# A hybrid trunk on one core: three mixer edits, other banks for the branch units, and another opening on TensorE

## The reference

```python
h = rms_norm(x, g_mix[l]);  u = h @ w_in[l]
y_pool = pool_mixer(u[..., OFF_POOL:OFF_CONV], pool_w[l], pool_scale[l])
y_conv = conv_module(u[..., OFF_CONV:OFF_Q], ...)   # GLU, 31 taps, LayerNorm, silu
y_attn = forgetting_attention(q, k, v, f_logit, ...) # 8 heads of 64, causal, with a bias per head and pair of tokens
gates = sigmoid(u[..., OFF_G:] + b_gate[l])          # 3 branches x 1024
merged = gates[0] * (y_pool @ w_br_pool) + gates[1] * (y_conv @ w_br_conv) + gates[2] * (y_attn @ w_br_attn)
x = x + merged @ w_out[l]
h = rms_norm(x, g_ffn[l])
x = x + (swiglu(h, ...) if l == 0 else moe_ffn(h, ...))   # dense 2816 wide, then top 2 of 8 experts, 3584 wide
```

## Time and profile before

| | |
|---|---|
| median of 3 runs | 1582.47 us (1580.74 to 1584.38) |
| the profiled execution's own time | 1584.88 us |
| its span, first to last instruction | 1583.1 us |
| granted TensorE clock, mean | 0.999 |
| TensorE matmul busy | 1566.5 us, 99% |
| VectorE busy | 1293.3 us, 82% |
| ScalarE busy | 1042.7 us, 66% |
| GpSimd busy | 32.8 us, 2% |

### The profile page before, as it was taken

The page is one execution under the profiler, slowest core; times in us unless marked ns, Lnnn a source line. Parts: engine busy times, 40 slices in busy tenths (PEclk is TensorE's granted clock), DMA queues, the critical chain, the costliest instruction groups (busy, mean ns, idle before and its releaser), DMA issues.

```text
span 1583.1 us, 22472 instructions
## 1 busy us (share of the span) xinstructions
PE 1566.5 (99%) x9385; PEld 1379.9 (87%) x9385; DVE 1293.3 (82%) x1137; ACT 1042.7 (66%) x957; POOL 32.8 (2%) x28
## 2 busy tenths in 40 slices
PE   9999999999999999999999999999999999999998
PEld 8999999999999998888888888888888888888887
DVE  6995885455898677998987988987988987988986
ACT  7546563344656568777677777777777777677675
POOL 1000200001000100000000000000000000000000
PEclk9999999999999999999999999999999999999999
DMA  9544555555554447999998999998999999999994
GB/s 318 183 134 145 180 182 187 185 185 187 161 159 140 157 157 270 357 366 358 376 369 325 372 371 361 371 372 322 374 370 357 372 373 338 364 360 378 364 364 184
DMA packets 182491, 453.12 MB, mean 286 GB/s; under 512 B 7168, under 2 KB 81024, under 8 KB 182272
## 3 DMA queue, kind: packets, MB, share of 16 engines
q1 hardware_dynamic: 182400, 451.82, 79.7%
HBM read 450.74 MB, written 1.05 MB: 285 GB/s over the span
## 4 chain that ended last, share of the span: by engine, by line
PE 93%; DVE 5%; ACT 1%; DMA 1%; issue 0%; SPq 0%; DVEq 0%; ACTq 0%
PE bank L317 29%; PE bank L318 28%; PE bank L319 28%; DVE w_low L307 2%; PE bank L1678 2%; PE bank L1656 1%; PE bank L1701 1%; DMA raw<-w_in 1%; ACT w_high L303 0%; PE bank L1411 0%; DVE y_low L814 0%; DVE h_full L804 0%; PE bank L1479 0%; PE bank L1457 0%; DVE h_low L797 0%
## 5 line engine op out<-in xcount | busy, mean ns | idle before, releaser
L307 DVE TENSOR_TENSOR w_low<-raw,w_high 128x2048 fp32r<-128x2048 f32 (+1 forms) x426 | 959.4, 2290 | 112.6 <-ACT w_high L303 111.8
L303 ACT ACTIVATE w_high<-raw 128x2048 fp32r<-128x2048 f32 (+1 forms) x426 | 804.4, 1919 | 157.4 <-DMA raw<-exp_w 155.8
L317 PE MATMUL bank<-w_high,hg_high 128*128 128x512 f32 x896 | 351.8, 393 | 1.4 <-DVE w_low L307 1.4
L319 PE MATMUL bank<-w_high,hg_low 128*128 128x512 f32 x896 | 349.1, 390 | 0.0
L318 PE MATMUL bank<-w_low,hg_high 128*128 128x512 f32 x896 | 348.9, 389 | 0.0
L317 PE MATMUL bank<-h_high,w_high 128*128 128x256 f32 x1024 | 290.8, 284 | 1.7 <-DVE h_low L797 1.6
L318 PE MATMUL bank<-h_low,w_high 128*128 128x256 f32 x1024 | 285.6, 279 | 0.0
L319 PE MATMUL bank<-h_high,w_low 128*128 128x256 f32 x1024 | 285.6, 279 | 0.0
L317 PEld LDWEIGHTS bank<-w_high,hg_high 128*128 128x128 f32 x896 | 168.3, 188 | 36.4 <-issue 1.2
L317 PEld LDWEIGHTS bank<-h_high,w_high 128*128 128x128 f32 x1024 | 194.1, 190 | 6.4 <-issue 3.8
L319 PEld LDWEIGHTS bank<-w_high,hg_low 128*128 128x128 f32 x896 | 168.2, 188 | 35.3
(11 more groups left out here) (296 smaller groups left out, 1591.6 us busy)
## 6 DMA issues: line engine op xcount, KB each, us to landing
raw<-exp_w SPq DMA_DIRECT2D x336, 1024.0 KB, 5.3
raw<-w_in SPq DMA_DIRECT2D x39, 1024.0 KB, 5.1
raw<-ffn_w SPq DMA_DIRECT2D x33, 1024.0 KB, 5.3
raw<-w_out SPq DMA_DIRECT2D x8, 1024.0 KB, 5.1
raw<-w_br_attn SPq DMA_DIRECT2D x4, 1024.0 KB, 5.0
raw<-w_in SPq DMA_DIRECT2D x2, 1056.0 KB, 7.5
raw<-w_br_pool SPq DMA_DIRECT2D x2, 1024.0 KB, 5.1
raw<-w_br_conv SPq DMA_DIRECT2D x2, 1024.0 KB, 4.8
```

What stands on the lines that cost most here:

```text
L303: nc.scalar.activation(slot(wh, c), slot(raw, c), ACT.Copy).then_inc(s["high_done"], 1)
L307: nc.vector.tensor_tensor(slot(wl, c), slot(raw, c), slot(wh, c).bitcast(F32), ALU.subtract).then_inc(s["split_done"], 1)
L317: pe.matmul(dst, lh, rh, start=start and i == 0, stop=False)
L319: last = pe.matmul(dst, ll, rh, start=False, stop=stop and i == len(terms) - 1)
```

## The change

- The branch units 21 to 32 go round banks 0, 1, 4, 5, 2 in place of 0, 1, 2. Unit 33 has bank 0 still, whose last owner is now unit 31 in place of unit 30.
- On ScalarE `attn_out` stands ahead of `gate_out` at n = 17, 19 and 21, and at n = 23 `gate_out(20)` stands right behind the layer norm's tanh, ahead of the copy of the conv branch.
- `pair_scores` starts with q by k, adds both diagonal masks in one matmul of 2 x 128 columns, and ends with the bias rows.
- The last of the four zero matmuls ahead of the dense layer's sums, that of bank 7, stands behind the sums.
- At the start 22 matmuls of 512 columns take the place of 15 and the block of 24 of several widths.

```diff
-UNIT_BANK = [0, 1, 2, 4, 5, 0, 1, 2, 4] + [u % 3 for u in range(9, UNITS - 1)] + [1]
+UNIT_BANK = [0, 1, 2, 4, 5, 0, 1, 2, 4] + [u % 3 for u in range(9, 21)] + [0, 1, 4, 5, 2, 0, 1, 4, 5, 2, 0, 1] + [0, 1, 2, 1]
...
                         nc.scalar.activation(cs[:], cv[:], ACT.Tanh, scale=0.5).then_inc(s["ln_th"], 1)
+                        gate_out(20)
                         act.wait_ge(s["y_full"], 2 * l + 2)
                         nc.scalar.activation(yH[:, 2:4, :], yf[:], ACT.Copy).then_inc(s["y_high_done"], 1)
                         attn_out(3)
                         attn_high(3)
-                        gate_out(20)
...
+                    if n in (17, 19, 21):
+                        attn_out((n - 17) // 2)
                     if 12 <= n <= 22:
                         gate_out(n - 3)
-                    if n in (17, 19, 21):
-                        attn_out((n - 17) // 2)
...
                     for a in range(2):
-                        B = bank[4 + a]
-                        pe.matmul(B[:, 0:384], sel8[:, 2 * j + a:2 * j + a + 1].to_broadcast([P, P]), crow[:], start=True, stop=False)
-                        pe.matmul(B[:, 0:128], identr[:], maskr[:], start=False, stop=False)
-                        pe.matmul(B[:, 256:384], identr[:], maskr[:], start=False, stop=False)
+                        rows = slice(64 * a, 64 * a + 64)
+                        pe.matmul(bank[4 + a][:, 0:128], qk[rows, j, 0:P], qk[rows, 4 + j, 0:P], start=True, stop=False)
                     for a in range(2):
                         rows = slice(64 * a, 64 * a + 64)
-                        pe.matmul(bank[4 + a][:, 0:128], qk[rows, j, 0:P], qk[rows, 4 + j, 0:P], start=False, stop=False)
+                        pe.matmul(bank[4 + a][:, 128:384], qk[rows, j, P:S], qk[rows, 4 + j, :], start=False, stop=False)
                     for a in range(2):
-                        rows = slice(64 * a, 64 * a + 64)
-                        pe.matmul(bank[4 + a][:, 128:384], qk[rows, j, P:S], qk[rows, 4 + j, :], start=False,
+                        pe.matmul(fold(bank[4 + a][:], 2)[:, :, 0:P], identr[:], maskr[:].unsqueeze(1).to_broadcast([P, 2, P]),
+                                  start=False, stop=False)
+                    for a in range(2):
+                        pe.matmul(bank[4 + a][:, 0:384], sel8[:, 2 * j + a:2 * j + a + 1].to_broadcast([P, P]), crow[:], start=False,
                                   stop=True).then_inc(s["scores"], 1)
...
-                            for m in range(4):
+                            for m in range(3):
                                 zero_bank(4 + m)
                             norm_stats(1)
+                            zero_bank(7)
...
-            keep_awake(15, 7, wh[5][:, 0:P], wh[5][:, 0:512])
-            still = hH[:, 0:2, :].rearrange("p a b -> p (a b)")
-            for n in (512, 128, 264, 384):
-                pe.matmul(bank[7][:, 0:n], wh[5][:, 0:P], still[:, 0:n], start=True, stop=True)
-                for at in (0, 0, P, 0, 0):
-                    pe.matmul(bank[7][:, 0:S], wh[5][:, at:at + P], still[:, 0:S], start=True, stop=True)
+            keep_awake(22, 7, wh[5][:, 0:P], wh[5][:, 0:512])
```

## The result

The kernel after takes 1578.76 us in the median of 20 runs (1571.61 to 1581.2); the kernel before, run beside it, 1586.03 us (20 runs, 1579.69 to 1590.75). The ratio is 0.9948 with a 95% interval of 0.9936 to 0.9959: 8.2 us less by the ratio, 7.3 by the two medians. The forecast was 5.8 us, 0.9963: the side is right, the size somewhat small. By the time alone rival (1) with its 7.4 us, 0.9953, would fit better, and the forecast lies outside the interval; only the traces can tell the two apart.

What follows compares the result with a forecast made beforehand. The prediction took TensorE to bound the kernel, with 93% of the chain that ended last. Values 2.3, banks 2.5 and scores 1.0 make 5.8 us, from 1582.47 to 1576.7 us, own range 1575.2 to 1578.4.

Steps and rivals of the forecast that it cites:

- rival (1): At the banks, VectorE does not lag, so they give 4.1 us; 7.4 us in all, 1575.1 us; chance 0.25.
- Values: 1.14 a layer: In pair_turn(3), copying values earlier removes the second three transposes' stall: 1.14 us a layer, 2.3 in two.
- idle + 0.17 + 0.11: For TensorE's waits, a stall costs more than its row's idle time: add 0.17 and 0.11 us.
- Banks, the removed stalls: 2.05 a layer: At units 23, 26 and 28, five banks remove stalls of 0.74, 0.64 and 0.67: 2.05 us a layer.
- Banks, given back: 0.8: At unit 33, TensorE stalls 0.7 with refill on merged_low, the next split takes 0.1, leaving 1.25 us a layer.
- near 3 us long: Sign to look for: VectorE's w_low split beside GpSimd's adds would be near 3 us long.
- (2): At the merge, VectorE's lag takes all the banks give; 3.3 us gained in all, 1579.2 us; chance 0.14.
- (3): VectorE sets the end of the merge, its lag growing past the whole gain; time 1586 us; chance 0.04.
- Scores: 0.5 a layer: In the pairs' score blocks, the reorder saves about 0.5 us a layer, 1.0 in two; bounds 0 and 2.0.
- Zeros and start: 0: At the dense layer's sums and the kernel's start, no gain: TensorE starts 0.8 us earlier but waits until 18.1.
- rival (4): At the start, TensorE's pauses drop the clock to 1.2 GHz; 1.3 us of gain, 1581.2 us; chance 0.05.
- Rival (5): The change fails: other waits replace those removed, or the masks cost double; 1582.5 us; chance 0.06.

Runs made afterwards that it cites:

- experiment 1: Kernel before with only attn_out moved ahead of gate_out at n = 17, 19, 21; 1583.11 us, ratio 0.9986.
- experiment 2: Kernel before with only the new bank table and gate_out(20) behind the tanh; 1583.62 us, ratio 0.9983.
- Experiment 10: Kernel after with a small memset in place of each of GpSimd's four adds, conv part not merged; 1573.55 us, ratio 0.9933.
- experiment 6: Kernel after with gate_out(20) back behind attn_high(3) as before; 1574.54 us, ratio 0.995.
- experiment 5: Kernel after with the first output piece's w_low split ahead of branch(25); 1578.74 us, ratio 0.9951.
- 9: Kernel after with the first output piece's split ahead of branch(25) and GpSimd's fourth add on VectorE behind branch(29); 1577.6 us, ratio 0.9942.
- experiment 3: Kernel before with only the scores reordered: q by k first, one mask matmul, bias rows last; 1583.68 us, ratio 0.9977.
- experiment 4: Kernel before with only the last zero matmul behind the sums and the new start; 1584.36 us, ratio 0.9993.
- experiment 11: Kernel after with the old zeros and old start, keeping values, banks and scores; 1579.54 us, ratio 0.9963.
- 12: Kernel after with the first output piece's split ahead of branch(25), two adds on GpSimd and two on VectorE; 1577.3 us, ratio 0.9931.
- 8: Kernel before run again unchanged for a second trace; 1585.54 us, ratio to itself 1.0005.
- 7: Kernel after run again unchanged for a second trace; 1572.7 us, ratio 0.9944.

## Why the prediction came out right

**Values: 1.14 a layer.** Measured 1.16 in either layer, read at the turn itself, and shown alone by experiment 1. The forecast took it from the distance of starts; its rule "idle + 0.17 + 0.11" would have given 1.25 here, where the matmuls are transposes of 128 columns.

**Banks, the removed stalls: 2.05 a layer.** Measured 2.10 and 2.08, and the same in experiment 2. For these the rule held: 0.75, 0.65 and 0.69 by it, 0.76, 0.64 and 0.70 measured.

**Banks, given back: 0.8.** Measured 0.87 and 0.85: 0.71 at unit 33 and the rest at the split behind it. That leaves 1.23 in either layer where I said 1.25. The mechanism was that of the forecast: the split of 3.06 us ("near 3 us long"), released at the end of GpSimd's second add, which came at 166.29. Experiment 10 takes the adds away and the stall goes; 6 takes VectorE's gain of 0.7 away and it doubles. Rival (1), no lag, falls with these, and so do (2) and (3), which wanted 2.05 or more. The Trainium skill, SBUF — State Buffer, "Who interferes with whom", says that GpSimd and a VectorE instruction with two SBUF inputs exclude each other instruction by instruction; the 3.06 and 2.28 us with and without the adds, and the 1.77 of experiment 5, agree. My expectations for experiments 5 and 9 used this rule for the split and forgot it for the add two rows on. (Of the eight adds in the earlier trace rows two are over 3.3 us long, one in each layer, and not one as the prediction has it; the argument stands.)

**Scores: 0.5 a layer.** Measured at the blocks 0.58 and 0.67 in the trace of after, 0.40 and 0.44 in experiment 3. TensorE's timeline after, pair 0 and pair 1, to be laid beside the earlier trace rows:

```profile
83.04 0.49 PE L1457 MATMUL bank<-h_full 64*128 64x128 f32 x4
83.34 0.63 PE L1460 MATMUL bank<-h_full 64*128 64x256 f32 x4
83.90 0.50 PE L1462 MATMUL bank<-mask_r,ident_r 128*128 128x256 f32 x2
84.24 0.52 PE L1465 MATMUL bank<-bias_rows,head_rows 128*128 128x384 f32 x2
...
95.57 0.49 PE L1457 MATMUL bank<-h_full 64*128 64x128 f32 x4
...
97.12 0.82 PE L1479 MATMUL bank<-cst,prob 128*128 128x128 f32 x6
```

The mask with repeated columns goes at full speed, 0.34 for two. Pair 1's block, first to next group, is 1.55 in place of 1.69.

**Zeros and start: 0.** TensorE's timeline of the start, after, beside the earlier trace rows:

```profile
2.15 7.98 PE L1298 MATMUL bank<-w_high 128*128 128x512 f32 x22 [2.15 <-DVE w_high L1274]
10.89 0.39 PE L317 MATMUL bank<-w_high,y_high 128*128 128x256 f32 x1 [0.76 <-DVE w_low L1279]
...
18.48 0.40 PE L317 MATMUL bank<-w_high,y_high 128*128 128x264 f32 x1 [0.80 <-DVE w_low L307]
```

The first product starts 0.22 earlier, not the 0.8 I had: its `w_low` was there 0.5 later than in the first trace of before. As forecast it doesn't matter: the second piece waits for VectorE (at 18.48; it stood at 18.16 before, and the forecast was 18.1). Behind both pauses the granted clock is 1.00 and a product steps by 0.12, so rival (4) falls. The trace of experiment 4 has nothing for the two edits together, and experiment 11 without them equals the kernel after; the 2.1 us between the upper groups of experiment 4 and before stay unexplained.

**The sum.** 5.8 us forecast, 5.82 over the two mixers in the traces. That the two agree to the hundredth is luck: the 5.82 hold 0.71 lost to a step outside the change, and 0.43 gained at the start and 0.2 behind the turn of layer 0, which no term has. The terms read at their own places make 2.3 + 2.5 + 1.25, about 6.0 us.

What the forecast lacked lies for the most part outside the change. The dense layer's step (-6.68) was drawn low in the profiled execution. It was drawn high in the output projection of layer 0 (+0.71, in both traces of after and in experiment 2, not in 5, 6, 9, 10, 11 and 12). One wait of the experts, at 1429.81, is in none of the other thirteen traces. In the many runs 8.2 us stand by the ratio, or 7.1 by groups. The 1.3 us above 5.8 stay open. The first trace of before lies 1.5 below the median of its own group (1584.88 against 1586.4), so other executions of that kernel may have waits that this trace doesn't show; that these make up the rest is argued and not shown.

The single parts show the same excess. Their 35 runs of before have 13 in a lower group (median 1580.7) and 22 in an upper one (1586.8). Upper group against upper group, experiments 1 to 4 are 3.7, 3.2, 2.2 and 2.1 us below before, where the terms read in their traces are 2.3, 2.5, 0.8 and 0. These four gains add up to more than the whole change. So the traces give the size of each part here, and the times of the runs confirm the side and no more. None of the 24 runs of experiments 1 and 2 is in a lower group, so a kernel's share of such runs may depend on the kernel too. Rival (5), no effect, falls with experiments 1 and 2.

## What to carry to other kernels

A stall removed from a bound engine is worth what the next engine's lead allows: count the lead of the engine that feeds it through every instruction up to the next place where they meet, and price each instruction that meets the other user of SBUF as held to the end of that one's instruction. Where two engines share such a job, give the slow one only as much as it ends before the fast one needs its own adds. Before believing a difference of two traces, look for the stretch that the change doesn't touch: here it held more than half.

## What the runs showed of the hardware that was not expected

- **Two step levels at one clock.** Matmuls of 256 columns with a weight load each step by 0.1133 or 0.1177 us for a whole stretch, with the granted clock at 1.00 in both. It is worth 6.68 us over 177 us of dense layer. The traces of the kernels before, 1, 2, 3, 4, 5, 8, 9, 11 and 12 have the upper level there, those of after, 6, 7 and 10 the lower. What draws it isn't settled. The level can change with no wait and no other kind of matmul between: within one unbroken row of products it fell at 68.5 us of the trace of after and at 446.8 of that of before, and rose at 543.9 in that of experiment 6.
- **A clock fall in light work.** In the routing stretch ahead of the experts the granted clock went to its low level in 7 of the 14 traces: 3.28 us lost in the trace of experiment 2, next to nothing in that of after, where the waits of 0.7 and 0.3 us that before has in the routing are gone (0.79 granted from 572 to 580 us).
- **A whole hold on a short instruction.** An add of VectorE of 0.69 us took 1.77 when it met a GpSimd add of 1.25 us at its start, and a split of 2.28 took 3.06.
